# First attention of a two-block network: when the score products of its two maps are issued

## The reference, cut to what matters

```
def block(args):
    q1b, q2b, start = args
    q_pos = start + jnp.arange(Q_BLOCK)
    causal = k_pos[None, :] <= q_pos[:, None]

    def probs(qb, k):
        s = jnp.einsum('bhqd,bhkd->bhqk', qb, k, preferred_element_type=jnp.float32) * scale
        return jax.nn.softmax(jnp.where(causal, s, -jnp.inf), axis=-1)

    attn = probs(q1b, k1) - lam * probs(q2b, k2)
    return jnp.einsum('bhqk,bhkd->bhqd', attn, v32)
```

## Time and profile before

| | |
|---|---|
| median of three runs | 2616.76 us (2604.16 to 2618.91) |
| profiled execution | 2615.4 us, its span 2613.6 us |
| TensorE matmuls busy | 2420.7 us, 93% of the span |
| VectorE, ScalarE, GpSimd busy | 1474.0, 796.7 and 1149.3 us |
| first attention, its exponentials | from 329.6 to 493.1 us |

### The profile page before, as it was taken

The page is one execution under the profiler, slowest core; times in us unless marked ns, Lnnn a source line. Parts: engine busy times, 40 slices in busy tenths (PEclk is TensorE's granted clock), DMA queues, the critical chain, the costliest instruction groups (busy, mean ns, idle before and its releaser), DMA issues.

```text
span 2613.6 us, 32997 instructions
## 1 busy us (share of the span) xinstructions
PE 2420.7 (93%) x11798; PEld 1966.8 (75%) x11798; DVE 1474.0 (56%) x2047; ACT 796.7 (30%) x1517; POOL 1149.3 (44%) x888
## 2 busy tenths in 40 slices
PE   7998667798899999999989998989989999999996
PEld 7976645577688888888868886768768888888885
DVE  5984556547456555555573511665645555556556
ACT  4221245524322222222242001553432222222222
POOL 3220040155456655555673443000735556556553
PEclk8998889899999999999999999999989999999999
DMA  5446510013111111111152113000311111111113
GB/s 143 125 130 149 160 62 1 1 57 121 45 53 60 48 48 48 49 60 53 44 193 58 49 49 121 1 1 28 127 45 50 59 53 56 48 48 48 52 57 145
DMA packets 176916, 179.30 MB, mean 69 GB/s; under 512 B 39704, under 2 KB 139544, under 8 KB 176816
## 3 DMA queue, kind: packets, MB, share of 16 engines
q1 hardware_dynamic: 171520, 164.02, 20.4%
q10 hardware_dynamic: 5296, 13.96, 1.5%
HBM read 147.46 MB, written 30.49 MB: 68 GB/s over the span
## 4 chain that ended last, share of the span: by engine, by line
PE 82%; DVE 6%; ACT 4%; DMA 3%; issue 3%; POOL 2%; SPq 1%; POOLq 0%; ACTq 0%; DVEq 0%
PE ps L267 23%; PE ps L268 23%; PE ps L269 23%; PE ps L1458 3%; PE ps L1488 3%; PE ps L1474 2%; ACT ex L1535 2%; PE ps L474 1%; DVE hbuf L425 1%; DMA msb<-ssm_lags 1%; DVE hbuf L1965 1%; PE ps L1463 1%; PE ps L2686 1%; PE ps L1349 0%; PE ps L456 0%
## 5 line engine op out<-in xcount | busy, mean ns | idle before, releaser
L1965 DVE TENSOR_TENSOR hbuf<-hbuf,ps 128x1024 f32<-128x1024 f32 x320 | 390.7, 1221 | 253.5 <-PE ps L269 231.7
L267 PE MATMUL ps<-mlp_dh,mlp_fh 128*128 128x512 f32 x672 | 264.4, 393 | 12.7 <-POOL mlp_dzl L1766 10.0
L269 PE MATMUL ps<-mlp_dh,mlp_fl 128*128 128x512 f32 x672 | 263.1, 392 | 0.0
L268 PE MATMUL ps<-mlp_dl,mlp_fh 128*128 128x512 f32 x672 | 262.6, 391 | 0.0
L207 POOL TENSOR_TENSOR wgt<-raw,ones 128x512 fp32r<-128x512 f32 x76 | 87.3, 1148 | 326.4 <-PE ps L269 165.6
L1753 POOL TENSOR_TENSOR mlp_s_raw<-mlp_gh_raw,mlp_s_raw 128x512 f32<-128x512 f32 x44 | 57.1, 1297 | 284.2 <-PE ps L269 284.2
L267 PEld LDWEIGHTS ps<-mlp_dh,mlp_fh 128*128 128x128 f32 x672 | 126.6, 188 | 43.6 <-POOL mlp_dzl L1766 10.8
L268 PEld LDWEIGHTS ps<-mlp_dl,mlp_fh 128*128 128x128 f32 x672 | 126.7, 189 | 27.5
L269 PEld LDWEIGHTS ps<-mlp_dh,mlp_fl 128*128 128x128 f32 x672 | 126.5, 188 | 27.7
L1458 PE MATMUL ps<-k,q 64*128 64x512 f32 (+6 forms) x416 | 86.8, 518 | 64.1 <-ACT ex L1535 62.8
L1766 POOL TENSOR_TENSOR mlp_dl<-mlp_d_raw,mlp_dh 128x1024 fp32r<-128x1024 f32 x42 | 113.8, 2710 | 46.5 <-ACT mlp_dh L1942 46.5
(11 more groups left out here) (484 smaller groups left out, 6776.8 us busy)
## 6 DMA issues: line engine op xcount, KB each, us to landing
h<-hbuf SPq DMA_DIRECT2D x24, 512.0 KB, 2.9
mlp_d_raw<-in_w_down SPq DMA_DIRECT2D x21, 512.0 KB, 3.4
mlp_d_raw<-in_w_ffn_out SPq DMA_DIRECT2D x21, 512.0 KB, 3.3
raw<-in_w_in SPq DMA_DIRECT2D x40, 256.0 KB, 2.7
raw<-in_w_out SPq DMA_DIRECT2D x32, 256.0 KB, 2.5
res_b<-h SPq DMA_DIRECT2D x16, 512.0 KB, 4.5
mlp_ul<-in_w_up SPq DMA_DIRECT2D x22, 256.0 KB, 3.0
mlp_uh_raw<-in_w_up SPq DMA_DIRECT2D x22, 256.0 KB, 3.4
```

Source lines behind the costliest of these rows:

```text
L267: pe.matmul(out, lhs[0], rhs[0], start=first, stop=False, skip_group_check=over)
L268: pe.matmul(out, lhs[0], rhs[1], start=False, stop=False, skip_group_check=over)
L269: return pe.matmul(out, lhs[1], rhs[0], start=False, stop=last, skip_group_check=over)
L1965: v.tensor_tensor(self.acc[:, i, :], self.acc[:, i, :], src, ALU.add).then_inc(self.s["added"], 1)
```

## The change

`pe_scores` no longer issues both maps in turn. For the first attention it waits for `exp0`, issues all chunks and masks of map 0, waits for `exp1`, and issues all chunks and masks of map 1. The loop over chunks is moved to a function of its own, `pe_score_parts`, which takes a list of parts (one for each map in the first attention; both heads of a pair at once in the second, as before).

```
             if self.maps == 2:
-                halves = [(n, m, h, self.s[f"s{m}"]) for m in range(2)]
-                if n >= 1:
-                    for m in range(2):
+                for m in range(2):
+                    if n >= 1:
                         pe.wait_ge(self.s[f"exp{m}"], n)
+                    self.pe_score_parts(pe, i, w, [(m, n, m, h, self.s[f"s{m}"])])
             else:
-                halves = [(n + m, 0, h // 2, self.s["s0"]) for m in range(2)]
                 if n >= 2:
                     pe.wait_ge(self.s["max0"], n)
+                self.pe_score_parts(pe, i, w, [(m, n + m, 0, h // 2, self.s["s0"]) for m in range(2)])
+
+        def pe_score_parts(self, pe, i, w, parts):
+
             for a in range(0, w, 512):
                 b = min(a + 512, w)
                 d0 = max(a, w - P)
-                for r, (item, m, t, done) in enumerate(halves):
+                for r, item, m, t, done in parts:
                     rows = slice(ST * r, ST * (r + 1))
                     pe.matmul(self.score(item, m, a, b), self.q[rows, t, i * P:(i + 1) * P],
                               self.k[rows, t, a:b], start=True, stop=True)
-                for item, m, t, done in halves:
+                for r, item, m, t, done in parts:
                     if d0 < b:
```

## The result

The kernel after takes 2704.48 us (median of 4 runs, 2697.93 to 2706.67), the kernel before on the same chips 2617.84 (2604.16 to 2620.18). The ratio is 1.0344, 95% interval 1.0322 to 1.0365: 87 us slower, where 26.7 were forecast and 2629 to 2653 us given as the range. The sign was right and the size was not. The profiled execution of after has a span of 2696.1 us, 82.5 more than before; it is the shortest of the four.

What follows compares the result with a forecast made beforehand. A loop of waits in the first attention, no engine full, was taken as the bound. Three heads at full clock lose 19.1 us and the first 7.6: 26.7 us, or 2643.5 us on the median, range 2629 to 2653.

Steps and rivals of the forecast that it cites:

- What bounds the loop: First attention: no engine is full; a loop of waits through scores, masks, transposes, products, copy and two exponentials sets the time.
- its terms: Per item of the first attention: longer by one map's score time plus 0.15 us less one exponential; 6.36 us a head.
- Lone products stream at a paired record's rate, with loads hidden: First-attention scores: one map alone takes as long as the pair did, 1.67 ns a column, weight loads under running records.
- the first rival: First-attention scores: a lone map streams at twice the rate, 0.21 us a record; 2611 us in all; chance 6%.
- the third: First-attention scores: a lone map's loads wait for the record ahead, some 0.19 us each; 2684 us; chance 3%.
- The second: First attention: the exponential waits for map 0's earlier maximum, not the copy; each item gains, 2597 us; chance 2%.
- the last: Other slack that could not be placed swallows the move; time within 10 us of before; chance 4%.
- Gap of 0.15 us: TensorE, first attention: time from map 0's lone mask to map 1's first score record, bounds 0.05 and 0.20 us.
- The early start's gain: First attention: map 0's scores start one exponential earlier, 0.37 to 1.01 us an item, 4.8 us a head.
- The clock: TensorE's granted clock: expected to hold at full in heads 2 to 4, since TensorE would be busy longer.
- TensorE stays at half clock: Rival: one map at a time keeps the clock from rising or lets it fall later; 2690 us and more; chance 4%.
- the first head's clock: First head, begun at half clock: loses 10.7 us if the clock rises as now, 4.5 if earlier; middle 7.6 taken.

Runs made afterwards that it cites:

- e4: TensorE alone, reference left out: nine stretches of 60 or more fp32 products on all rows, half rows, pairs or mixes; sixty took 54 us on all rows, 102.8 on half.
- e1: Kernel after, but each first-attention score product runs over all 128 rows, with the other map's query rows zeroed: 2621.13 us, ratio 1.0027 to before.
- e3: Kernel after, but map 0's scores wait for both exponentials; the maps still come one after the other: 2729.04 us, ratio 1.0432 to before.
- e8: e1, but map 0's scores wait for both exponentials, as in e3: 2653.36 us, ratio 1.0135 to before.
- e5: TensorE alone, five stretches begun at full clock: all rows, half rows, pairs with rests; half rows without rests, with or without masks. Half rows with 1.36 us rests fell.
- e2: Kernel before, but each pair of first-attention score products is issued twice: 2660.87 us, ratio 1.0177 to before.
- e9: Kernel before, unchanged, run again for a second profile: 2618.63 us.
- v2: e1, but in items of more than one batch the first transposes and value products precede the scores of item n+2: 2608.94 us, ratio 0.9974 to before.
- e6: Kernel before with the change for the items of 144, 272 and 400 columns alone: 2633.24 us, ratio 1.0085 to before.
- e7: Kernel before with the change for the item of 1040 columns alone: 2631.04 us, ratio 1.0069 to before.

## Why the prediction was wrong, point by point

- *What bounds the loop*: right. The early start and the longer scores moved the loop as the prediction has it; at full clock the intervals of 784 and 912 columns grew by 0.62 and 0.83 us, where its terms give 0.76 and 0.87.
- *Lone products stream at a paired record's rate, with loads hidden*: right. 1.52 and 1.73 us, and 0.88 us a product in e4. This puts out the first rival (twice the rate) and the third (loads out of hiding). The second (the earlier maximum pulls the exponential ahead) and the last (other slack swallows the move) would have given 2597 us or a time within 10 us of before, and 2704 came.
- *Gap of 0.15 us*: right, 0.16. That most of it goes with the change between 64 and 128 rows came out of e1 (0.03 to 0.06 without one).
- *The early start's gain*: 19 us forecast; 23 (give or take 11) between e3 and after, 28 (give or take 7) between e8 and e1. The surplus of the second pair goes with the falls of the clock that e8 has and e1 hasn't.
- *The clock*: this is the step that failed. The prediction gave "TensorE stays at half clock" 4%, with the reason "the clock held at 1.00 through stretches with TensorE busy 71% of the time, and it will be busy longer", and it let the first head's clock rise the same or earlier, since TensorE would have fewer pauses. It took the busy share for what holds the clock. The pairs of before used all 128 rows of the array in the scores; the lone products use 64. e4 and e5 show that such work never raised the clock from half, and lost it where a rest of 1.36 us stood beside it. The kernel after has idle times of 0.2 to 1.2 us before its scores, other work on all rows between them, and no run shows how much of each it takes. In its first head, which was to gain from fewer pauses and lose 7.6 us in all, the clock did not rise until 373 us, and the head lost 21.9. In e1, on all rows, the clock rose at 335.1 us and stayed.
- *Price of that rival*: 2690 us "and more"; 2704 came. That the number is so near is partly luck: it had heads 2 to 4 at half clock throughout and nothing more for the first, while they ran so for a third to three quarters of their time and the first head lost 14.3 us beyond its forecast. The chance was too low.

The Trainium skill, "TensorE: Matmul & The Clock Gate", Part 1, says that the clock follows "how busy the PE has been recently". By that rule this change looked safe. The trace doesn't agree: 23.9 us of 23.9 busy at 0.50, and 102.8 us of unbroken work in e4.

Shown: half rows keep the clock down where all rows let it rise, and with rests of 1.36 us they lose it where all rows keep it (e4, e5); with the order and waits of after, all rows cost 8 us instead of 87 (e1), and with those of e3 37 instead of 116 (e8). Shown too: half rows are not the only cause of a fall. Behind idle times of 1.3 to 2.2 us it comes on pairs and on all rows (e2, e8, e9), and in v2 behind shorter ones. Not separated: how much of the 83 us between after and e1 is the clock, and how much the changes between 64 and 128 rows that e1 saves as well. The 784-column item, at full clock in both, says 0.35 us an item of the latter (6.44 in after, 6.09 in e1), over 32 items 11 us; the head of e1, 42.7 against the 47.2 of the forecast, says 4.5 us a head or 18. By these estimates 65 to 72 are clock, which counts also the first head, where e1's clock rose earlier than before's. It stays open when exactly a given head falls: e6, e7, e9 and v2 show that the same code does and does not.

## What to carry to other kernels

Before two products that share the array by rows are pulled apart, count them twice: they stream one after the other, and the array is then half used for twice as long, which the granted clock may answer by halving, with TensorE busy throughout. Read PEclk beside the busy share in every stretch that an edit touches, and distrust a gain or loss of some 10 us in a stretch with idle times of 1 to 2 us between short groups of work, since the clock may fall in one head and not in the next. Where a short contraction must run alone, padding it with zeros to all rows cost no stream time here. It kept the clock where the waits were short (e1), not behind idle times of 2.15 us (e8).

## What the runs showed of the hardware that was not expected

- Sixty lone fp32 products of 512 columns on 64 rows took 102.8 us, on 128 rows 54.1, and sixty pairs 54.6 (e4).
- Zero weights in half of the rows, and using 64 of the 128 columns, let the clock rise (54.1 and 53.7 us for sixty): of the unbroken work that was tried, only unused rows held it down.
- A pair and a lone product in turn rose from rest to full clock (54.2 us); a product on all rows and one on 64 in turn did not (120.3 us). The latter takes 17.5 us more than sixty half-row products at the same clock, 0.29 us for each of sixty products: the change of rows at half clock, averaged over both ways.
- At full clock a 64-row product starts 0.16 us after a 128-row mask; a 128-row product starts 0.03 to 0.06 after it.
- Once down, the clock was up again within a few us on all rows (0.51 and then 0.99 in e8, around 463.4 us) and on pairs (0.50 and then 0.99 in e9, around 355.1), while on 64 rows it stayed at 0.50 through 23.9 us without a pause (after) and 102.8 us (e4).
